# State inputs in eight buffers, two more PSUM banks and a new order at the head of a hybrid mixer

## What is computed

```python
def ssd_scan(xh, dt, A, Bm, Cm, h0, with_output):
    ...
    a_cs = jnp.cumsum(a, axis=-1)
    decay_states = jnp.exp(a_cs[..., -1:] - a_cs)
    states = jnp.einsum('bclhn,bhcl,bclhp->bchpn', Bc, decay_states, x)
    ...
q = rmsnorm(u[..., :ATTN_DIM].reshape(Bsz, L, ATTN_HEADS, HEAD_DIM), q_norm_w)
...
qx = apply_axial_rope(qx, rope)
```

## Time and profile before

| | us |
|---|---|
| median of 3 runs | 1632.84 |
| lowest, highest | 1632.81, 1634.03 |
| the profiled execution | 1635.75 |
| its span, first to last instruction | 1633.9 |
| TensorE busy in it | 1563.0 (96%) |
| VectorE busy | 871.9 (53%) |
| ScalarE busy | 589.9 (36%) |
| GpSimd busy | 156.0 (10%) |

### The profile page before, as it was taken

One profiled execution on the slowest core, in us unless ns is written; L12 is line 12 of the kernel. 1 busy time (PEld: TensorE's weight loads), 2 busy tenths in 40 slices (PEclk: granted clock), 3 DMA queues, 4 the chain that ended last, 5 costly groups with the idle time before them and its releaser, 6 DMA issues.

```text
span 1633.9 us, 22386 instructions
## 1 busy us (share of the span) xinstructions
PE 1563.0 (96%) x9110; PEld 1413.1 (86%) x9110; DVE 871.9 (53%) x1182; ACT 589.9 (36%) x896; POOL 156.0 (10%) x156
## 2 busy tenths in 40 slices
PE   6999878999999999999999999997899999999999
PEld 4899767799899999999999998986788788888887
DVE  4687775545665554555544368456556434333333
ACT  6634444543622211222112245354555422222223
POOL 0321153011000000000000023014101000000000
PEclk8999999999999999999999999999999999999999
DMA  9555100012353333333331123220013233333322
GB/s 370 165 177 182 40 1 1 1 52 65 120 164 109 125 127 129 118 114 129 129 121 58 52 79 85 66 65 1 1 40 94 74 99 94 90 98 95 90 86 82
DMA packets 203581, 154.76 MB, mean 95 GB/s; under 512 B 8612, under 2 KB 189676, under 8 KB 203372
## 3 DMA queue, kind: packets, MB, share of 16 engines
q1 hardware_dynamic: 202060, 148.85, 29.3%
q10 hardware_dynamic: 1440, 4.78, 0.9%
HBM read 151.52 MB, written 2.10 MB: 94 GB/s over the span
## 4 chain that ended last, share of the span: by engine, by line
PE 84%; DVE 9%; ACT 5%; issue 2%; POOL 0%; DMA 0%; SPq 0%; DVEq 0%; ACTq 0%
PE banks L1763 68%; PE banks L1881 6%; PE banks L2031 1%; PE banks L1998 1%; PE banks L1907 1%; PE banks L1975 1%; DVE w_lo L1209 1%; DVE mod_sum L1234 1%; DVE neg_max L1569 1%; PE banks L2012 1%; DVE nrm L1311 1%; DVE h_lo L1305 1%; PE banks L1976 1%; PE banks L1715 1%; DVE qk L1439 1%
## 5 line engine op out<-in xcount | busy, mean ns | idle before, releaser
L1209 DVE TENSOR_TENSOR w_lo<-raw,w_hi 128x1056 fp32r<-128x1056 f32 x184 | 245.4, 1334 | 307.5 <-ACT w_hi L818 306.7
L1763 PE MATMUL banks<-h_hi,w_hi 128*128 128x384 f32 (+3 forms) x1296 | 389.6, 359 | 15.4 <-ACT silu_a L1147 6.5
L1763 PE MATMUL banks<-h_lo,w_hi 128*128 128x384 f32 (+3 forms) x1296 | 385.0, 355 | 0.0
L1763 PE MATMUL banks<-h_hi,w_lo 128*128 128x384 f32 (+3 forms) x1296 | 384.3, 355 | 0.0
L818 ACT ACTIVATE w_hi<-raw 128x1056 fp32r<-128x1056 f32 x184 | 198.5, 1079 | 253.9 <-PE banks L1763 231.4
L1763 PEld LDWEIGHTS banks<-h_hi,w_hi 128*128 128x128 f32 x1296 | 237.5, 190 | 45.3 <-issue 11.9
L1763 PEld LDWEIGHTS banks<-h_hi,w_lo 128*128 128x128 f32 x1296 | 239.3, 190 | 17.0
L1763 PEld LDWEIGHTS banks<-h_lo,w_hi 128*128 128x128 f32 x1296 | 239.5, 190 | 16.0
L1763 PE MATMUL banks<-g_hi,w_hi 128*128 128x384 f32 (+1 forms) x528 | 160.1, 357 | 0.0
L1763 PE MATMUL banks<-g_hi,w_lo 128*128 128x384 f32 (+1 forms) x528 | 159.2, 355 | 0.0
L1763 PE MATMUL banks<-g_lo,w_hi 128*128 128x384 f32 (+1 forms) x528 | 158.8, 355 | 0.0
(11 more groups left out here) (209 smaller groups left out, 1930.9 us busy)
## 6 DMA issues: line engine op xcount, KB each, us to landing
raw<-in_w_dram SPq DMA_DIRECT2D x120, 512.0 KB, 4.0
mod_ring<-in_w_mod_dram SPq DMA_DIRECT2D x96, 512.0 KB, 5.0
raw<-in_w_in_dram SPq DMA_DIRECT2D x32, 512.0 KB, 4.7
raw<-in_w_out_dram SPq DMA_DIRECT2D x16, 512.0 KB, 4.1
raw<-in_w_dram SPq DMA_DIRECT2D x16, 384.0 KB, 3.5
x_in<-in_x_dram ACTq DMA_DIRECT2D x4, 512.0 KB, 7.6
out_dram<-x_out SPq DMA_DIRECT2D x8, 256.0 KB, 2.3
inv_n<-in_count_dram ACTq DMA_DIRECT2D x4, 400.0 KB, 3.1
```

The costliest lines, as they stand in the source:

```text
L1209: dve.tensor_tensor(w_lo[n % 2][:, :], raw[n % 4][:, :], as_f32(w_hi[n % 2][:, :]), ALU.subtract).then_inc(lo_ready, 1)
L1763: ins = pe.matmul(to(p, a, b), ws[:, w], xs(k, a, b), start=(first and q == 0), stop=(last and q == 2))
```

## The change

It touches the mixer's head in both layers. The cs event moves ahead of the k transposes, and the rotation of block 1 gets an event of its own, ("rot1",), behind them. ("q23",1) and ("q23",2) move behind the first four states, which now follow ("tr","q",0) directly, and ("q23",3) moves behind the two states of unit 1. x_w gets eight buffers, at the place of e_in and e_cum, which the scan's chunks use later. The first four states go to banks 0, 1, 4 and 5, the others to 4 and 5 in turn. The waits follow: only state 2 waits for the evacuated pool results, a state's product waits for the last but one only from the fifth on, GpSimd waits for TensorE only from the ninth x_w on, the first scores wait for two copied states, pool 0 no longer waits for the column sums' evacuation, and its own evacuation no longer waits for pool 1. The number of instructions of each kind stays.

```diff
+XW = 8
...
-        x_w = put("x_w", [P, 2, 256], at=S0 + 21504)
+        x_w = put("x_w", [P, XW, 256], at=S0 + 9216)
...
-            ev = [("tr", "x", 0), ("tr", "x", 1), ("tr", "b", 0), ("tr", "k", 0), ("tr", "k", 1), ("cs",), ("q23", 0),
-                  ("pool", 0), ("pool", 1), ("q23", 1), ("tr", "q", 0)]
-            ev += states[:2] + [("q23", 2)] + states[2:4] + [("q23", 3)]
+            ev = [("tr", "x", 0), ("tr", "x", 1), ("tr", "b", 0), ("cs",), ("tr", "k", 0), ("tr", "k", 1), ("rot1",), ("q23", 0),
+                  ("pool", 0), ("pool", 1), ("tr", "q", 0)]
+            ev += states[:4] + [("q23", 1), ("q23", 2)]
...
+                if u == 1:
+                    ev.append(("q23", 3))
...
+        def state_bank(n):
+
+            return (0, 1, 4, 5)[n] if n < 4 else 4 + n % 2
...
-                        if n_st >= 2:
-                            pool.wait_ge(st_pe, l * INCS["st_pe"] + n_st - 1)
-                        pool.tensor_tensor(x_w[:, n_st % 2, :].rearrange("p (h q) -> p h q", h=HEADS),
+                        if n_st >= XW:
+                            pool.wait_ge(st_pe, l * INCS["st_pe"] + n_st - XW + 1)
+                        pool.tensor_tensor(x_w[:, n_st % XW, :].rearrange("p (h q) -> p h q", h=HEADS),
...
-                        act.wait_ge(pm_pe, l * INCS["pm_pe"] + 2)
+                        act.wait_ge(pm_pe, l * INCS["pm_pe"] + e[1] + 1)
...
-                    if e == ("cs",):
+                    if e == ("rot1",):
                         rotate(1)
...
-                            dve.tensor_copy(h_prev[:, d, nxt, :], banks[:, 4 + n_st % 2, 0:256]).then_inc(st_ready, 1)
+                            dve.tensor_copy(h_prev[:, d, nxt, :], banks[:, state_bank(n_st), 0:256]).then_inc(st_ready, 1)
...
-                        pe.wait_ge(cs_ready, l * INCS["cs_ready"] + 3)
+                        if e[1]:
+                            pe.wait_ge(cs_ready, l * INCS["cs_ready"] + 3)
...
-                        pe.wait_ge(pm_out, l * INCS["pm_out"] + 2)
+                        if n_st == 2:
+                            pe.wait_ge(pm_out, l * INCS["pm_out"] + 2)
                         pe.wait_ge(xw_ready, l * INCS["xw_ready"] + n_st + 1)
-                        if n_st >= 2:
+                        if n_st >= 4:
                             pe.wait_ge(st_ready, l * INCS["st_ready"] + n_st - 1)
-                        pe.matmul(banks[:, 4 + n_st % 2, 0:256], b_tok[:, cc, :], x_w[:, n_st % 2, :], start=True, stop=True)\
+                        pe.matmul(banks[:, state_bank(n_st), 0:256], b_tok[:, cc, :], x_w[:, n_st % XW, :], start=True, stop=True)\
...
-                        elif u:
-
+                        elif u == 0:
+
+                            pe.wait_ge(st_ready, l * INCS["st_ready"] + 2)
+                        else:
                             pe.wait_ge(exp_ready, l * INCS["exp_ready"] + (u if u < two_buffers else u - 1))
```

More of the change, by code:

```diff
@@ L1554, in _ @@
                             dve.wait_ge(st_pe, l * INCS["st_pe"] + n_st + 1)
-                            dve.tensor_tensor(h_prev[:, d, nxt, :], h_prev[:, d, nxt, :], banks[:, 4 + n_st % 2, 0:256], ALU.add)\
+                            dve.tensor_tensor(h_prev[:, d, nxt, :], h_prev[:, d, nxt, :], banks[:, state_bank(n_st), 0:256], ALU.add)\
                                 .then_inc(st_ready, 1)
```

## The result

The changed kernel takes 1640.31 us (median of 16 runs, 1636.89 to 1644.06) against 1633.94 of the kernel before (16 runs, 1629.4 to 1638.29). The ratio is 1.0036 with a 95% interval of 1.0026 to 1.0045: slower, by some 6 us. The profiled span is 1638.7 us, with as many instructions of each compute engine as before.

A forecast was written before the change was run, and what follows sets the result against it. No engine full in the mixer heads; a chain of short steps, mostly VectorE's, bounds them. Delays of 2.5 and 2.9 us sum to 5.4 at low clock, 2.3 at full; 4.6 taken on 1632.84 gives 1637.4, range 1632.0 to 1640.8.

The forecast's parts named there:

- GpSimd meets the sine part after x_w 3: Mixer head: only four x_w can be prepared ahead, not eight, leaving TensorE idle about 7 us before state 4.
- state 4's start at 212.0: Layer 0 head: sine part 208.8 to 211.3, x_w 4 to 211.9, then TensorE starts state 4.
- The scaling's end: Layer 0 head: VectorE scales the last q only after state 3, ending at 208.75 where it was 203.65.
- state 2's add: Mixer head: VectorE's add follows state 2's start by 0.78 us, in layer 0 at 204.0.
- The rotation beside GpSimd's x_w: Layer 0 head: GpSimd's x_w beside the first rotation and sum of squares were to add 0.1 us.
- the S1 scores: Mixer head: at the lower clock S1's maxima follow the scores' start by 2.81 us; full clock needs about half.
- the two bounds of 2.3 and 5.4: Total delay of both heads: 5.4 us at the lower clock throughout, 2.3 with the clock full; 4.6 taken.
- whole: Behind the head: the delay of S2's maxima passes on undiminished, as exponential of unit 2 precedes e_cum without a gap.
- B: Rival: same delayed chain in the heads but the clock full, +2.3 us, 1635.1; chance 0.25.
- C: Rival: S2's delay doesn't reach the chunk loop but S1's gain does, -2.0 us, 1630.8; chance 0.15.
- D: Rival: VectorE and GpSimd port holds at full price on top of the forecast, +7.6 us, 1640.4; chance 0.10.
- Nothing uses: Mixer head: S0's maxima may go 3 us earlier without use, since S1's scores queue behind state 4 on TensorE.

The follow-up runs named there:

- e1: Changed kernel with only the sine part of the last q moved behind the states of unit 0: 1633.74 us, ratio 0.9989 to the kernel before.
- e6: Changed kernel with GpSimd starting x_w 0 only after the first rotation: 1640.59 us, ratio 1.0037 to the kernel before.
- e4: Changed kernel with column sums and w_state again behind the k transposes and first rotation: 1635.06 us, ratio 1.0000 to the kernel before.
- b2: Kernel of b1 with the last q's rotation one unit later, behind the exponential of unit 2: 1629.88 us, ratio 0.9973 to the kernel before.
- b1: Changed kernel with column sums late, scaling before the q transpose, sine part behind unit 0's states: 1632.67 us, ratio 0.9991 to the kernel before.
- e8: Kernel before with only the last q's rotation moved behind the exponential of unit 2: 1635.34 us, ratio 0.9996.
- e2: Changed kernel with scaling before the q transpose and sine part between states 1 and 2 again: 1639.88 us, ratio 1.0030 to the kernel before.
- e7: Changed kernel with six unread products on TensorE between S0 and state 4: 1640.56 us, ratio 1.0036 to the kernel before.

## Why the prediction held, point by point

**The chain.** The forecast's main point was that GpSimd meets the sine part after x_w 3. The trace shows it (four x_w, 8.67 us of waiting, sine part, six x_w), and e1, which moves this event alone, takes the 6.6 us back. In layer 0 the forecast named state 4's start at 212.0 on the old trace; it came at 18.67 after b_tok, which is 212.18 there. The scaling's end was forecast at 208.75 and came at 208.83; cs_tok's end was forecast at 195.83 and came there. That the scaling fits so well is partly luck: the rotation took 0.65 us more than stood in the sum, and in e6, which takes just that away, the scaling ends at 208.07 on the old trace, so the other steps came some 0.6 us sooner than forecast. In layer 1 nothing made up for it. There states 2 and 3 also ran at the lower clock (0.50 granted from 1106 to 1111), and state 2's add followed 1.33 us after its start where 0.78 stood in the sum:

```profile
1106.01 2.07 PE L1961 MATMUL banks<-x_w,b_tok 128*128 128x256 f32 x4 [0.56 <-ACT mix L1046]
```

The scaling ended 0.73 us and state 4 started 0.69 us later than forecast, counted from b_tok.

**Terms that were off.** The rotation beside GpSimd's x_w was given 0.1 us and cost 0.75 (1.68 + 1.52 against 1.21 + 1.23); in layer 1 also 0.75. In e6, where the x_w wait, it takes 1.22 + 1.22 again. The Trainium skill's page "SBUF — State Buffer", section "SBUF: two separate sides", says that a VectorE instruction with two SBUF inputs and a GpSimd instruction that reads SBUF can't have their shared port pair at once; by this, the traces agree. In the other direction, the S1 scores were given 2.81 us at the lower clock. The clock was indeed low from 206 to 213, but was full again when the scores began at 213.63, and they took 1.49; in layer 1 they took 1.63. That is the term that was mis-sized: the old stretch ended 5.5 us after TensorE resumed, the new one 3.5 us after. By the granted clock the old one had begun 1.3 us before TensorE resumed and the new one 3.2 us before, which a forecast that counts from the resumption leaves out. Together: heads +1.4 and +2.2 where +2.5 and +2.9 stood; 3.6 in place of 5.4 (and of the 4.6 taken), between the two bounds of 2.3 and 5.4.

**What was missing.** The prediction passed the head's delay on "whole" and nothing more. The mixers lost another 3.8 us behind the heads, 2.1 and 1.7, going with two low-clock stretches that the text didn't have. (Of the 2.1 in layer 0, the second chunk's e_cum shows 1.3; where the other 0.8 went was not found.) So the total came near its number, 6.4 us by the medians against 4.6, with one term too large and one absent. The forecast is right in the mechanism and partly by luck in its size. The median of 1640.31 also lies only 0.5 us under the upper end of the range, and the kernel before took 1633.94 in these runs, 1.1 us more than the 1632.84 that the forecast started from.

**Rivals.** B, the clock full throughout, is out (0.61 granted from 205 to 212), though layer 0's S1 scores did run at the full clock, as it had them. C, slack in the first turn of the chunk loop, is out: e_cum starts at 31.47 after b_tok where it started at 30.09, the whole 1.4 us later. D, the port at full price, named 1640.4, and the median is 1640.31, nearer to it than to the forecast's own 1637.4. The rows don't bear it out as the sum of its terms. Its holds came to some 2.0 us of the 3 on VectorE's path (the rotation 0.65 more than taken in each layer; one multiply of 0.85 us in place of 0.42 behind state 4, and in layer 1 one of 0.73), but they are inside the 3.6 us of the heads, where D had 7.6; and e6, without the rotation's part, is no faster in the median. Its number was hit by what was lost behind the heads. "Nothing uses" the earlier maxima of S0 held: they came 3.0 us earlier (15.24 against 18.25 after b_tok).

**What stays open.** Why the clock falls behind the gate's root in layer 1 in the changed kernel (both traces) and in nine of the ten variants (all but e1), and not in the kernel before, is not settled: the idle time ahead of it is 1.90 us in either. TensorE there, changed kernel and then before:

```profile
1178.93 1.73 PE L2059 MATMUL banks<-tab,gn_r 128*128 128x128 f32 x8 [1.90 <-DVE gn_r L1617]
```

```profile
1175.53 1.16 PE L2048 MATMUL banks<-tab,gn_r 128*128 128x128 f32 x8 [1.90 <-DVE gn_r L1610]
```

The times of e1, e4 and e6 don't follow from their heads alone. e4 got back 2.8 us in the heads, 4.7 in the mixers as wholes and 5.3 in the median; e1 3.0, 4.9 and 6.6; e6 1.35, 1.3 and nothing. The sorting of all traces by their low stretches (83.4 against 85.1 us in layer 1) ties the loss behind the heads to them, but no run fixed the clock through a whole mixer, so that loss was seen and not tested. The new PSUM banks and the waits that went with them were never run without the rest of the change, so their share is not known.

## What to carry to other kernels

Where all engines walk one list, a deeper buffer is filled only up to the next instruction in the producer's queue that waits for something late: look for that one before counting buffers, and move it behind the train. Work that nobody waits for, brought forward, can delay work that somebody waits for, by its place in the queue and by the port it shares. And a chain's engine has gaps further on (here VectorE's wait for e_cum): an instruction moved there from between two maxima can be nearly free. That has to be measured in place: in b2 the move gained 2.8 us over b1, in e8 nothing over the kernel before.

## What the runs showed of the hardware that was not expected

The same idle time of TensorE was not always followed by the same clock. In the first chunk 0.73 and 1.96 us of it stood in all eight traces with the rotation between the maxima of S1 and S2, and in six of them TensorE then ran at 1.2 GHz for some 3.5 us (in the changed kernel e_cum of the second chunk starts 10.0 us after the first in place of 8.7); in e2 and e4 it didn't. Idle time of 1.90 us ahead of the gate's products was followed by the lower level in both traces of the changed kernel and by the full one in both of the kernel before. So the idle time right before a row doesn't decide it alone, and a head that was earlier by 2.5 us (b1) had the same stretch in the first chunk as one that was later by 1.4. Filling one gap (e7) kept the clock full there without any gain in the end. And a multiply of two tiles that takes VectorE 0.42 us took up to 1.10 in the changed kernel beside GpSimd's product, and four x_w took GpSimd 4.29 us beside VectorE's rotation and 2.32 alone (e6).
